# Causal attention on three 128x128 blocks: the mask added by TensorE, softmax read from PSUM, reciprocals in the transposing product

## The reference

```python
# first block, each of 2 layers: MLA (8 heads, 96-wide queries and keys) and MoBA (8 heads of 64)
s = einsum('bhqd,bhkd->bhqk', qb, k) * scale
s = where(kpos <= qpos, s, -inf)            # causal; 256 queries x 256 keys per head
p = softmax(s, axis=-1)
o = einsum('bhqk,bhkd->bhqd', p, v)
# second block, layer 1: grouped-query attention, 8 heads of 128, 2 key/value heads,
# 256 queries against 512 keys (tokens and context), no mask
```

## Time and profile before

| | |
|---|---|
| median of 3 runs | 3087.2 us (3084.85 to 3090.15) |
| profiled execution | 3093.44 us, its span 3091.5 us |
| busy share of the span | PE 91%, DVE 56%, ACT 36% |
| mean granted PE clock | 0.953 |
| attention of b1, layers 0 and 1 | 245.7 to 356 us, 895.8 to 1005 us |
| attention of b2, layer 1 | 2791 to 2846.5 us |

### The profile page before, as it was taken

How to read it: one execution, slowest core, us unless ns; L and a number is a source line. 1 busy time by engine, 2 the same in 40 slices (tenths; PEclk the granted TensorE clock), 3 DMA queues, 4 the chain that set the end, 5 groups by cost and what they waited for, 6 DMA issues and landing times.

```text
span 3091.5 us, 37932 instructions
## 1 busy us (share of the span) xinstructions
PE 2820.6 (91%) x15524; PEld 2327.4 (75%) x15524; DVE 1733.5 (56%) x2438; ACT 1107.4 (36%) x1661; POOL 0.2 (0%) x4
## 2 busy tenths in 40 slices
PE   6887899998977999989999899999989999877998
PEld 4665688896755879977878674888867888665898
DVE  3579636653889347655545424564554644455554
ACT  2344415643435246532222322222232222323443
POOL 0000000000000000000000000000000000000000
PEclk8998899998989999999999999999999999989999
DMA  6541155655331456636453221443335543220453
GB/s 266 196 169 55 62 177 207 230 179 199 127 116 55 150 196 224 208 115 239 150 180 134 101 68 61 142 152 130 135 109 203 179 136 119 72 82 21 148 182 115
DMA packets 122460, 447.42 MB, mean 145 GB/s; under 512 B 13488, under 2 KB 14640, under 8 KB 121904
## 3 DMA queue, kind: packets, MB, share of 16 engines
q1 hardware_dynamic: 122288, 445.00, 41.7%
HBM read 443.90 MB, written 1.05 MB: 144 GB/s over the span
## 4 chain that ended last, share of the span: by engine, by line
PE 78%; DVE 14%; DMA 3%; ACT 3%; issue 2%; SPq 0%; DVEq 0%; ACTq 0%
PE ps L532 21%; PE ps L533 20%; PE ps L534 20%; PE ps L536 16%; DMA ring<-stream 3%; DVE area L1445 3%; DVE area L1623 2%; DVE rests L1345 1%; DVE stat L1476 1%; DVE rs L1408 1%; DVE work L1485 1%; DVE work L1472 1%; PE ps L715 1%; DVE area L1416 1%; DVE h_split L1422 0%
## 5 line engine op out<-in xcount | busy, mean ns | idle before, releaser
L532 PE MATMUL ps<-h_split,heads 128*128 128x256 f32 (+1 forms) x2992 | 1015.4, 339 | 106.4 <-DVE h_split L1422 61.0
L533 PE MATMUL ps<-h_split,heads 128*128 128x256 f32 (+1 forms) x2992 | 989.9, 331 | 0.0
L534 PE MATMUL ps<-h_split,rests 128*128 128x256 f32 (+1 forms) x2992 | 988.6, 330 | 0.0
L1345 DVE TENSOR_TENSOR rests<-ring,heads 128x1024 fp32r<-128x1024 f32 x520 | 627.6, 1224 | 404.5 <-ACT heads L1003 396.9
L1003 ACT ACTIVATE heads<-ring 128x1024 fp32r<-128x1024 f32 x520 | 536.5, 1056 | 619.6 <-DMA ring<-stream 302.5
L532 PEld LDWEIGHTS ps<-h_split,heads 128*128 128x128 f32 x2992 | 590.4, 197 | 207.0 <-DVE h_split L1422 69.5
L533 PEld LDWEIGHTS ps<-h_split,heads 128*128 128x128 f32 x2992 | 592.1, 198 | 48.2 <-issue 3.6
L534 PEld LDWEIGHTS ps<-h_split,rests 128*128 128x128 f32 x2992 | 590.9, 197 | 46.2
L532 PE MATMUL ps<-hid_split,heads 128*128 128x256 f32 (+1 forms) x1056 | 365.3, 346 | 0.0
L534 PE MATMUL ps<-hid_split,rests 128*128 128x256 f32 (+1 forms) x1056 | 355.1, 336 | 0.0
L533 PE MATMUL ps<-hid_split,heads 128*128 128x256 f32 (+1 forms) x1056 | 354.8, 336 | 0.0
(11 more groups left out here) (161 smaller groups left out, 2267.8 us busy)
## 6 DMA issues: line engine op xcount, KB each, us to landing
ring<-stream SPq DMA_DIRECT2D x836, 512.0 KB, 3.4
consts<-constants SPq DMA_DIRECT2D x1, 1920.0 KB, 11.5
x_sb<-x_in SPq DMA_DIRECT2D x1, 1024.0 KB, 9.6
x_sb<-ctx_in SPq DMA_DIRECT2D x1, 1024.0 KB, 4.7
out<-area SPq DMA_DIRECT2D x1, 1024.0 KB, 4.8
cols<-columns SPq DMA_DIRECT2D x1, 695.5 KB, 4.2
consts<-constants SPq DMA_DIRECT2D x1, 674.5 KB, 10.9
sg<-positions_in SPq DMA_DIRECT2D x1, 128.0 KB, 10.7
```

Source lines behind the costliest of these rows:

```text
L532: nc.tensor.matmul(out, lhsT[0], rhs[0], start=first, stop=False)
L533: nc.tensor.matmul(out, lhsT[0], rhs[1], start=False, stop=False)
L534: ins = nc.tensor.matmul(out, lhsT[1], rhs[0], start=False, stop=last)
L1345: nc.vector.tensor_tensor(rests[:, u % RING, :], ring[:, u % RING, :], as_f32(heads[:, n % HEADS_RING, :]), ALU.subtract)\
```

## The change

- A causal head has only the three blocks of scores that are not masked throughout: queries 0 to 127 with keys 0 to 127 (in columns 0 to 127 of the bank), and queries 128 to 255 with all keys (columns 128 to 383). `keys_of` gives these columns.
- The mask shrinks to one triangle of 128x128. PE adds it with a product of the identity and the mask, accumulated on each of the two diagonal blocks. PE waits once for the tables.
- DVE takes the maximum from PSUM itself, one instruction for each b below J, and ACT takes the exponential from PSUM and writes `probs`. The add and the copy into `probs` are gone. The scores' bank is now free when the exponential is done.
- DVE no longer scales the probabilities. It scales the 128x128 identity by the reciprocals, one for each b below J, into `shares` (the buffer `sg2`, idle here), and PE multiplies the probabilities' blocks by that diagonal in place of the transposition: three plain float32 products in b1, four in b2. The wait for the transposition of t-2 moves from `first(t)` to just ahead of this step in `second(t)`.
- ACT copies, and PE multiplies by the values, three blocks in b1 in place of four.

```diff
-          ("mask", 512), ("g_v", 512), ("b_s", 512))
+          ("mask", P), ("g_v", 512), ("b_s", 512))
+        shares = sg2
...
-                        order = transposed_order(p)
-                        for b in range(4):
-                            ins = nc.tensor.transpose(out[:, order[b] * P:(order[b] + 1) * P],
-                                                      probs[:, s % 2, b * P:(b + 1) * P], mat("ident"))
-                        ins.then_inc(tensor_done, T.mark((p, "pt", s)))
+                        rows_of = share_of(p)
+                        for b, r in enumerate(rows_of):
+                            product(out[:, b * P:(b + 1) * P], probs[:, s % 2, b * P:(b + 1) * P],
+                                    shares[:, s % 2, r * P:(r + 1) * P], True, True,
+                                    (p, "pt", s) if b == len(rows_of) - 1 else None)
...
+                        keys = slice(0, (b + 1) * P)
-                            q, k = qt[:, t, b * P:(b + 1) * P], kt[:, t, :]
+                            q, k = qt[:, t, b * P:(b + 1) * P], kt[:, t, keys]
...
-                        product(out[:, b * SEQ:(b + 1) * SEQ], q, k, True, True, ((p, "at"), "s", t) if b else None)
+                        product(out[:, b * P:(2 * b + 1) * P], q, k, True, False)
+                        product(out[:, 2 * b * P:(2 * b + 1) * P], mat("ident"), mat("mask"), False, True,
+                                ((p, "at"), "s", t) if b else None)
...
-                    for b in range(2):
-                        product(held[0][r:r + 64, 0:SEQ], v[:, b, hh * 64:(hh + 1) * 64],
-                                probs_t[:, s % 2, b * SEQ:(b + 1) * SEQ], b == 0, b == 1,
+                    for i, (b, k) in enumerate(((0, 0), (1, 0), (1, 1))):
+                        product(held[0][r:r + 64, b * P:(b + 1) * P], v[:, k, hh * 64:(hh + 1) * 64],
+                                probs_t[:, s % 2, i * P:(i + 1) * P], k == 0, k == b,
...
+                pe.wait_ge(tables_landed, 16)
...
-                    nc.scalar.activation(probs[:, t % 2, b * W:(b + 1) * W], probs[:, t % 2, b * W:(b + 1) * W],
+                    keys = keys_of(J, b)
+                    nc.scalar.activation(probs[:, t % 2, keys], bank((p, "s", t))[:, keys],
...
+                A.found[("read", (p, "s", t))] = A.found[(p, "e", t)]
...
-                        nc.scalar.activation(probs_t[:, s % 2, :], bank((p, "pt", s)), ACT.Copy)\
+                        W = P * len(share_of(p))
+                        nc.scalar.activation(probs_t[:, s % 2, 0:W], bank((p, "pt", s))[:, 0:W], ACT.Copy)\
...
-                    if t >= 2:
-                        dve.wait_ge(tensor_done, after(T, (p, "pt", t - 2)))
-                    pr = probs[:, t % 2, :]
-                    if masked:
-                        step(nc.vector.tensor_tensor(pr, bank((p, "s", t)), mat("mask"), ALU.add), ("read", (p, "s", t)))
-                    else:
-                        step(nc.vector.tensor_copy(pr, bank((p, "s", t))), ("read", (p, "s", t)))
-                    step(nc.vector.tensor_reduce(st[:, 4:4 + J], pr.rearrange("p (j w) -> p j w", w=W), AX.X, ALU.max))
+                    for b in range(J):
+                        nc.vector.tensor_reduce(st[:, 4 + b:5 + b], bank((p, "s", t))[:, keys_of(J, b)], AX.X, ALU.max)\
+                          .then_inc(vector_done, V.mark())
+                    own()
...
+                    if t >= 2:
+                        dve.wait_ge(tensor_done, after(T, (p, "pt", t - 2)))
                     for b in range(J):
-                        o = probs[:, t % 2, b * W:(b + 1) * W]
-                        step(nc.vector.tensor_scalar(o, o, st[:, 6 + b:7 + b], None, ALU.mult),
-                             (p, "p", t) if b == J - 1 else None)
+                        nc.vector.tensor_scalar(shares[:, t % 2, b * P:(b + 1) * P], mat("ident"), st[:, 6 + b:7 + b],
+                                                None, ALU.mult)\
+                          .then_inc(vector_done, V.mark((p, "p", t) if b == J - 1 else None))
...
-def transposed_order(p):
-    return (0, 2, 1, 3) if p[0][0] == "b1" else (0, 1, 2, 3)
+def share_of(p):
+    return (0, 1, 1) if p[0][0] == "b1" else (0, 0, 0, 0)
+
+def keys_of(J, b):
+    return slice(b * P, (2 * b + 1) * P) if J == 2 else slice(0, TOK)
```

More of the change, by code:

```diff
@@ L1628, in _ @@
                 dve.wait_ge(tables_landed, 16)
-                attention((p, "at"), 16, 2, lambda t: (NOPE + ROPE_A) ** -0.5 if t < HEADS else 64 ** -0.5, True, taps)
+                attention((p, "at"), 16, 2, lambda t: (NOPE + ROPE_A) ** -0.5 if t < HEADS else 64 ** -0.5, taps)
                 dve.wait_ge(tensor_done, after(T, (p, "lnm")))
@@ L1707, in _ @@
                     head_norm((p, "k"), 2, kt, lambda c: col("gk2"), lambda e: mat("cos_c"), lambda e: mat("sin_c"))
-                    attention((p, "at"), 16, 1, lambda t: 128 ** -0.5, False)
+                    attention((p, "at"), 16, 1, lambda t: 128 ** -0.5)
                 T_ = TOK if l == 0 else SEQ
@@ L1801, in _constants @@
     m["sin_c"] = np.concatenate([np.sin(ang), np.zeros((P, SEQ))], 1)
-    mask = np.zeros((P, 2, SEQ))
-    for q in range(2):
-        mask[:, q, :] = np.where(np.arange(SEQ)[None] <= (q * P + np.arange(P))[:, None], 0.0, MASKED)
-    m["mask"] = mask.reshape(P, 2 * SEQ)
+    m["mask"] = np.where(np.arange(P)[None] <= np.arange(P)[:, None], 0.0, MASKED)
     pick1, pick2 = np.zeros((P, 2)), np.zeros((P, 4))
```

8 lines of the change are left out of this document (3 added, 5 removed).

## The result

The changed kernel takes 3045.69 us (median of 4 executions, 3040.14 to 3049.36), the kernel before 3086.89 us beside it. The ratio is 0.9861, 95% interval 0.9849 to 0.9873; a second time, on another chip, it was 0.9864 (0.9848 to 0.9881). The profiled execution was 3043.82 us.

A forecast was written before the change was run, and what follows sets the result against it. DVE was taken to bound b1's attention, and a closed loop through PE and DVE b2's. Savings of 24.0 us in b1, 8.7 in b2 and 0.5 for tables sum to 33.2, from 3087.2 to 3054.0 us; range 3045 to 3067.

The forecast's parts named there:

- A: Whole kernel: the gains come as worked out, 3054 us, between 3046 and 3063; chance 0.78.
- DVE in b1, first: Attention of b1: the two maxima take 0.74 us in place of 1.44 for add and maximum, 0.70 saved a turn.
- DVE in b1, second: Attention of b1: two scalings of the identity take about 0.55 us in place of 0.78, 0.23 saved a turn.
- the turn of 5.12 us: DVE in b1's attention: a turn goes from 6.05 to 5.12 us by the savings of 0.70 and 0.23.
- The cheap bound for the maxima: DVE in b1: the second maximum overlaps the first as the taps do, 0.06 each; 0.68 us, 0.76 saved.
- How many turns count: Each layer of b1: DVE leads for 14 first parts and 13 second parts, 12.8 us saved.
- The 0 behind the last gate: End of b1's attention: PE and ACT lead in either kernel, changes about cancel, 0 us.
- 13 turns, 7.15: b2, first transposition to that of task 13: 13 turns at 2.68 us, 0.55 less than 3.23 each, save 7.15 us.
- B: b1: PE's path around gates becomes the bound, 8 to 16 us of the gain lost, 3062 to 3070 us; chance 0.10.
- C: b1's gates: PE stays at the 1.2 GHz level, stall 5.6 us at eight gates, 3099 us, slower; chance 0.03.
- D: b1 and b2: a plain 128-column product costs 0.47 us, far dearer than a transposition, 3075 us; chance 0.04.
- E: Behind b1: the stream is the bound, PE waits for weights, both layers' 24 us lost, 3078 us; chance 0.05.

The follow-up runs named there:

- e1: Changed kernel with DVE waiting for itself behind each maximum and each scaling of the identity, three new waits a turn of b1; 3053.89 us, ratio 0.9897.
- g1: e2 plus products that nothing reads in b1: six ahead of the last transposing products, five ahead of the layer norm's second sums; 3034.31 us, ratio 0.9824.
- e4: Changed kernel with the mask added twice by PE, four more passes of 128 columns a turn of b1; 3050.86 us, ratio 0.9885.
- after: The changed kernel's first profiled execution, nothing else altered; 3043.82 us, with a median of 3045.69 us over its 4 executions.
- e2: Changed kernel, but in b2 alone DVE scales the probabilities and PE does the real transposition as before; 3042.36 us, ratio 0.9856.
- f1: The changed kernel run again unaltered, as yardstick; 3045.13 us, ratio 0.9864.
- f4: Changed kernel with the real transposition in both blocks, DVE scaling the probabilities; 3041.24 us, ratio 0.9855.
- g3: e2 with the layer norm's first sums in b1 moved ahead of the last task's transposing products, into PE's wait; 3030.47 us, ratio 0.9806.
- g4: g3 plus three products that nothing reads in the pause of 1.5 us ahead of the second sums; 3027.54 us, ratio 0.9798.
- f2: Changed kernel with ten products that nothing reads in b1, in PE's wait for the last task's shares; 3045.69 us, ratio 0.9867.
- f3: e2 and f2 together: real transposition in b2, ten products that nothing reads in b1; 3042.10 us, ratio 0.9857.
- e3: Changed kernel with DVE's copy of the scores into SBUF and its wait put back, maximum and exponential reading the copy; 3075.33 us, ratio 0.9971.
- g2: f4 with each transposition of b1 done twice into the same place; 3038.83 us, ratio 0.9836.

## Why the prediction was right or wrong

The mechanism was as forecast, A: DVE sets b1, the closed loop goes in b2, PE bounds what is left. The size was short by 7.8 us (33.2 against 41.0), which put the time just below the range. The range's low end counted 3 us for gates that meet a faster PE; no run shows such a gain. By its own steps, layer 0 of b1:

| step | forecast | measured | from |
|---|---|---|---|
| DVE in b1, first | 14 x 0.70 = 9.8 | 15 x 0.80 = 12.0 | first turn 4.78 to 3.98 |
| DVE in b1, second | 13 x 0.23 = 3.0 | 14 x 0.38 = 5.3 | turn 6.05 to 4.86 less the 0.80 |
| wait for the transposition at the last gate | 0 | 0.6 | 0.88 gone, some 0.3 new ahead of the shares |
| first scores | -0.4 | -0.4 | from the stretch's start to the first reading of scores 13.04 to 13.48 |
| stalls at gates | -0.4 | -0.7 | and the row at 295.98 |
| behind the last maxima | 0 | -1.2 | 17.13 to 18.33 |
| sum | 12.0 | 15.6 (15.5 in the table) | |

**The step that failed is the turn of 5.12 us**, the two terms "0.70 saved" and "0.23 saved". Widths were right: maxima from PSUM at 0.289 and 0.412, forecast 0.28 and 0.42; scalings at 0.284, forecast 0.29; the 512-column maximum from PSUM 0.691 against 0.686 from SBUF. What was wrong is the space between: a gap of 0.04 was added, at the scalings also ahead of the taps, where the instructions overlap by 0.08. The cheap bound for the maxima had the right mechanism (0.68) and was still above the measured 0.65: it read an overlap of 0.06 from eight taps in 3.38 us, but DVE waits for itself once among these eight, behind the first four. Four taps without a wait show the 0.08, (4 x 0.480 - 1.67) / 3:

```profile
247.82 1.67 DVE L1627 SCALAR_TENSOR_TENSOR area<-area,cols 128x256 f32<-128x256 f32 x4
```

The cheap bound for the scalings (0.50) was 0.10 above 0.40, since it kept the gap to the taps. The sizes alone are 14 x 0.10 + 13 x 0.15 = 3.4 us a layer, and with both cheap bounds it would still have been 1.9 short. e1 shows it: with three waits put back the turn is 5.25.

**How many turns count** was one short. DVE leads through the last gate as well: the wait of 0.88 us that made that place PE's in layer 0 of the kernel before was for the transposition, and the change itself moved it away (1.2 us for the turn, 0.6 for the wait).

**The 0 behind the last gate** was wrong by 1.2 us a layer (1.5 in layer 1) the other way, and for a cause that it did not name. With both sums at the high clock the place takes 15.4 to 15.7 us (both layers of e1 and g1, layer 0 of e4), some 1.6 less than before; with both slow 18.3 to 18.8 (after, e2, f1, f4), in e4's layer 1 19.7. Eleven of the traces have the pause of 2.5 us ahead of the second sums: of their 22 tails 8 have the sums in under 2.0 us, 12 in 3.4 to 3.65, two between. With a pause of at most 1.51 us (g1, g3, g4) they are fast in six of six, and with products in the wait ahead of the last shares (f2, f3, g1) so are the first sums, in six of six (2.0 us or less in six of 18 tails without them). This speaks for the pauses having a part in it, but the two layers of an execution often come out alike, so it rests on three executions. What decides it where the pause is there is open. The Trainium skill ("TensorE: Matmul & The Clock Gate", Part 1) says of a kernel's start that the same kernel shows a different number of slow products from run to run. Behind these pauses the traces show that in part: f2 and f3, with the same b1, differ, and so do the two layers of e4; but the changed kernel's b1, seen in three traces (after, f1, e2), was slow in six tails of six.

**b2** gave 9.9, forecast 8.7. Turn 2.64 (2.68), start 0.9 (1.1), tail 0.5 (0.4). The term that was off is "13 turns, 7.15": PE's first turn has no values yet and takes 1.82 us, so 13 turns gave 8.4. **Tables**: 0.44 for 0.5.

**The rivals.** B (gates bound b1): DVE waited at one of the eight gates, 0.65 us (in f1 at one, 0.62), not 1 to 2 us at each. C (slower by the clock at the gates): no; the longest such wait in any trace without e3's copy is f4's 1.60 us, far from the 4.2 at which it decides. D (a dear product): eight passes in 0.89 us, as worked out; a factor of two against the transposition, not the four of the Trainium skill ("TensorE: Matmul & The Clock Gate", Terms). It was nevertheless b2's bound, and e2 shows what the prediction left unsaid: the diagonal is a loss of 6.3 us there and only in b1 a gain, 0.07 us a turn by f4's 4.93; what more f4's one trace lost at gates is not seen in the whole times. E (given back behind b1): no; the rest came out within what it does in all kernels. The weighing of DVE's reads from PSUM went as the trace had it: 0.691 against 0.686 us; by the 62 cycles of the Trainium skill ("VectorE: DVE Perf Modes", the section on the TRN2 errata) each maximum would, as an estimate, have been 0.065 longer. The trace does not agree.

## What to carry to other kernels

Removing a wait between two small instructions of one engine saved more than the gap that the trace shows for it (0.13 us here, the gap 0.035): read how far pairs without a wait overlap, and take the gap out of the estimate at both ends. Ask of each engine what it does while another sets the pace: the same trade (a diagonal product on PE for a scaling on DVE) gained a little where DVE was full (a turn of 4.86 us in place of 4.93) and lost where PE was (2.64 in place of 2.19). A wait of PE close to the end of a stage is a place for a step whose input is ready; in g3 it saved its own time, and what followed ran at the high clock.

## What the runs showed of the hardware

- Two DVE instructions without a wait between them overlap by 0.08 us at 128 to 256 columns; with a wait of the engine for itself there is a gap of 0.035 us instead, and each such wait cost 0.13 us (0.39 for three, e1).
- Less work on PE went with a lower clock: with transpositions for the diagonal products in b1 the granted clock of its two attentions was 0.89 and 0.89, where 16 layers with the products had 0.92 to 0.99; the same transpositions done twice had 0.99 and 0.97 (f4 and g2, one trace each).
- Eight passes of 256 columns took 1.97 us (8 cases) or 3.4 to 3.65 us (12; two between) behind the same pause of 2.5 us, and 1.97 to 1.99 each time behind pauses of 1.51 us or less.
- ACT's exponential of 128x512 took 0.683 us from PSUM, and 0.722 from SBUF (e3, and the kernel before).
- DVE's maximum over 128x512 took 0.691 us from PSUM and 0.686 from SBUF.
